# Early planes for two back projections, cumulative decay rows read back from DRAM, and 128-row first tiles in a two-block fp32 layer

## The reference

```python
def first_block(x, w_in, b_f, conv_w, pool_w, pool_scale, w_out, ln_g, ln_b):
    proj = jnp.einsum('bsd,de->bse', x, w_in[l])          # 2048 -> 7176 columns
    (q, k, v, g_att, fg, c_b, c_c, c_h, g_conv, p_u, g_pool) = jnp.split(proj, IN_SPLITS, axis=-1)
    y_att  = forgetting_attention(q, k, v, fg, b_f) * silu(g_att)   # 8 heads of 128, logits + cum_q - cum_k
    y_conv = short_conv_mixer(c_b, c_c, c_h, conv_w) * silu(g_conv)
    y_pool = multiscale_pool_mixer(p_u, pool_w, pool_scale) * silu(g_pool)
    y = jnp.einsum('bse,ed->bsd', concatenate([y_att, y_conv, y_pool]), w_out[l])
    return layer_norm(DEEPNORM_ALPHA * x + y, ln_g, ln_b)

def second_block(x, ...):
    u = jnp.einsum('bsd,de->bse', h, w_in[layer])
    q, k, v, z_attn, q_idx, k_idx, w_idx, z_ssd, xbc, dt_raw = _split_cols(u, IN_WIDTHS_2)
    o_attn = _dsa_attention(q, k, v, q_idx, k_idx, w_idx) * silu(z_attn)   # top-128 keys by an index score
    o_ssd  = _ssd_mixer(xbc, z_ssd, dt_raw, ...)                           # 16 heads in 4 groups, chunks
    sub = jnp.einsum('bse,ed->bsd', concatenate([o_attn, o_ssd]), w_out[layer])
    return layer_norm(DEEPNORM_ALPHA_2 * h + sub, ln_g, ln_b)
```

## Time and profile before

| | |
|---|---|
| median of 3 runs (1828.44 to 1828.81) | 1828.46 us |
| profiled execution: time, span | 1829.15 us, 1827.4 us |
| PE busy | 1764.4 us, 97% of the span |
| PE weight loads busy | 1415.2 us, 77% |
| DVE / ACT / POOL busy | 1002.7 / 574.9 / 714.4 us |
| mean granted TensorE clock | 0.991 of full speed |
| chain that ended last: PE / DVE / ACT | 75% / 20% / 2% |
| DMA | 175.55 MB, 96 GB/s |

### The profile page before, as it was taken

How to read it: one execution, slowest core, us unless ns; L and a number is a source line. 1 busy time by engine, 2 the same in 40 slices (tenths; PEclk the granted TensorE clock), 3 DMA queues, 4 the chain that set the end, 5 groups by cost and what they waited for, 6 DMA issues and landing times.

```text
span 1827.4 us, 22151 instructions
## 1 busy us (share of the span) xinstructions
PE 1764.4 (97%) x7938; PEld 1415.2 (77%) x7938; DVE 1002.7 (55%) x1382; ACT 574.9 (31%) x796; POOL 714.4 (39%) x303
## 2 busy tenths in 40 slices
PE   7999999999999999999899999999989999999996
PEld 6877778788888887888778777777748777778885
DVE  4344333333322645113678989897599766576326
ACT  5322222322222224123632333333362323251211
POOL 3433333343444444443344324343314333325445
PEclk9999999999999999999899999999999999999998
DMA  5322222222333323332433222232212222217422
GB/s 200 114 81 81 81 82 92 81 81 81 99 103 92 97 95 131 116 126 69 163 93 114 69 70 93 62 88 81 69 36 92 81 69 69 80 58 252 126 83 92
DMA packets 50091, 175.55 MB, mean 96 GB/s; under 512 B 5217, under 2 KB 5473, under 8 KB 48865
## 3 DMA queue, kind: packets, MB, share of 16 engines
q1 hardware_dynamic: 41472, 152.13, 26.8%
q10 hardware_dynamic: 8544, 22.37, 3.4%
HBM read 166.09 MB, written 8.39 MB: 95 GB/s over the span
## 4 chain that ended last, share of the span: by engine, by line
PE 75%; DVE 20%; ACT 2%; issue 2%; POOL 1%; DMA 0%; ACTq 0%; DVEq 0%; SPq 0%; POOLq 0%
PE bank L330 73%; DVE gate L1065 3%; DVE feats L1053 2%; DVE bias L1053 2%; DVE bias L1553 1%; PE bank L334 1%; DVE top L1549 1%; DVE probs L1053 1%; DVE gT L1415 1%; DVE gate L1097 1%; DVE nmax L1092 1%; DVE tmp L1053 1%; DVE probs L1104 1%; DVE wide L1408 1%; POOL w_lo L308 1%
## 5 line engine op out<-in xcount | busy, mean ns | idle before, releaser
L308 POOL TENSOR_TENSOR w_lo<-raw,w_hi 128x1024 fp32r<-128x1024 f32 x280 | 688.8, 2464 | 1096.7 <-ACT w_hi L718 1096.7
L330 PE MATMUL bank<-planes_hi,w_hi 128*128 128x512 f32 (+1 forms) x1792 | 709.7, 396 | 19.0 <-DVE w_lo L1128 9.4
L330 PE MATMUL bank<-planes_lo,w_hi 128*128 128x512 f32 (+1 forms) x1792 | 694.8, 388 | 0.0
L330 PE MATMUL bank<-planes_hi,w_lo 128*128 128x512 f32 (+1 forms) x1776 | 687.7, 387 | 0.0
L718 ACT ACTIVATE w_hi<-raw 128x1024 fp32r<-128x1024 f32 x280 | 296.9, 1060 | 909.6 <-PE bank L330 893.3
L330 PEld LDWEIGHTS bank<-planes_hi,w_hi 128*128 128x128 f32 x1792 | 339.7, 190 | 110.2 <-issue 36.6
L330 PEld LDWEIGHTS bank<-planes_lo,w_hi 128*128 128x128 f32 x1792 | 340.1, 190 | 70.2 <-issue 4.8
L330 PEld LDWEIGHTS bank<-planes_hi,w_lo 128*128 128x128 f32 x1776 | 336.2, 189 | 68.3
L330 PE MATMUL bank<-w_hi,planes_hi 128*128 128x512 f32 x512 | 199.9, 391 | 4.2 <-DVE planes_lo L1069 4.2
L330 PE MATMUL bank<-w_hi,planes_lo 128*128 128x512 f32 x512 | 199.2, 389 | 0.0
L330 PE MATMUL bank<-w_lo,planes_hi 128*128 128x512 f32 x512 | 199.2, 389 | 0.0
(11 more groups left out here) (252 smaller groups left out, 1376.5 us busy)
## 6 DMA issues: line engine op xcount, KB each, us to landing
raw<-in_stream SPq DMA_DIRECT2D x282, 512.0 KB, 3.6
h_rows<-feats ACTq DMA_DIRECT2D x4, 1024.0 KB, 7.0
feats<-in_x_t SPq DMA_DIRECT2D x3, 1024.0 KB, 10.5
bias<-in_x_rows ACTq DMA_DIRECT2D x2, 1024.0 KB, 6.2
probs<-in_x_rows ACTq DMA_DIRECT2D x2, 1024.0 KB, 8.4
bias<-h_rows ACTq DMA_DIRECT2D x2, 1024.0 KB, 6.7
probs<-h_rows ACTq DMA_DIRECT2D x2, 1024.0 KB, 8.0
out<-feats ACTq DMA_DIRECT2D x6, 256.0 KB, 2.9
```

The lines of the kernel that those rows point to most:

```text
L308: nc.gpsimd.tensor_sub(w_lo[:, s, :], raw[:, s, :], w_hi[:, s, :].bitcast(fp32)).then_inc(lo_ready, 1)
L330: return nc.tensor.matmul(o, a, b, start=start, stop=stop)
```

## The change

Five things.

1. `EARLY = 4`: ACT cuts the first four planes of each back projection while PE is in the last forward tile before it (`cut_early`), and DVE their low parts.
2. In block 1 the `cum` matrix is stored to DRAM once, and ACT issues a DMA per head that reads the head's row into all 128 partitions (`load_cum_row`). The matmul that spread it and DVE's masking are gone; `logit_bias` reads SBUF.
3. The misc tile and SSD tile 0 are made in parts of 128, 128 and 256 tokens (`project_part`).
4. Of the four transposed banks per row block ACT scales three, DVE one.
5. `prepare` runs after SSD tile 2 and the decay spread after tile 3, both with what DVE does for them; its rows are in `bias`, not in `probs`.

The head loop of block 1 on ACT and the last turn of that of block 2 on ACT and DVE are written out. Lines are those of the diff's two sides; what is left out repeats these edits or only adds and renames semaphores.

```diff
-BACK_ORDER = [list(range(12)) + [15, 14, 13, 12], list(range(8, 16)) + list(range(8))]
+BACK_ORDER = [list(range(12)) + [15, 14, 13, 12], list(range(4)) + list(range(8, 16)) + list(range(4, 8))]
+EARLY = 4
...
-            def turn_and_spread(h):
+            def turn_head_v(h):
                 pe.wait_ge(acc_taken, T_HEAD1 + 4 * h + 3)
                 turn_v(M, vT)
-                pe.wait_ge(cum_row_ready, h + 1)
-                if h:
-                    pe.wait_ge(feat_done, h)
-                mm(O[:, :], ones[0:HEADS, :], cum_row[0:HEADS, :]).then_inc(cum_spread, 1)
...
             pe.wait_ge(rows_taken, 14)
-            project_half(tile_at(T_MISC, 0), 0, T_MISC - SK - 1)
+            project_part(tile_at(T_MISC, 0), 0, 1, T_MISC - SK - 1)
             turn_rows(2)
-            project_half(tile_at(T_SSD, 0), 0)
+            project_part(tile_at(T_SSD, 0), 0, 1)
+            project_part(tile_at(T_MISC, 0), 1, 1)
             turn_rows(3)
-            project_half(tile_at(T_MISC, 0), 1)
-            project_half(tile_at(T_SSD, 0), 1)
+            project_part(tile_at(T_SSD, 0), 1, 1)
+            project_part(tile_at(T_MISC, 0), 2, 2)
+            project_part(tile_at(T_SSD, 0), 2, 2)
...
                 ssd_tile(6 * it + 1)
-                if g < 0:
-                    prepare()
-                else:
+                if g >= 0:
                     ssd_states(g)
                     ssd_spread(g, 0)
                 ssd_tile(6 * it + 2)
                 if g < 0:
-                    spread_decay()
+                    prepare()
...
+            def load_cum_row(a):
+                act.dma_start(cum_rows, cum_dram[a:a + 1, :].to_broadcast([P, S])).then_inc(cum_loaded, 16)
...
+            def cut_early(blk, first):
+                act.wait_ge(unit_used, 2 * first - 1)
+                act.wait_ge(feat_done, 24 * blk + EARLY)
+                for n in range(EARLY):
+                    cut_hi(BACK_ORDER[blk][n], 16 + 32 * blk + n + 1)
...
-            act.wait_ge(cum_ready, 1)
+                if j == 1:
+                    act.wait_ge(cum_ready, 1)
+                    act.dma_start(cum_dram, cumT[0:HEADS, :]).then_inc(cum_stored, 16)
+                if j == 2:
+                    act.wait_ge(cum_stored, 16)
+                    load_cum_row(0)
             exp_gate(1)
-            with step.loop(1, HEADS, 0) as h:
+            for h in range(1, HEADS):
                 head_exps(h - 1)
+                load_cum_row(h)
...
-                        if b < 2:
+                        if b < 3:
                             act.wait_ge(rows_turned, n)
...
-            back_and_norm(0, T_BACK1, x_rows, {1: lambda: turn_round(tile_at(T_POOL, 7))})
+            back_and_norm(0, T_BACK1, x_rows, {EARLY: lambda: turn_round(tile_at(T_POOL, 7))})
...
                 t = tile_at(T_HEAD2, 1, h, 2)
-                turn_round(t)
+                if isinstance(h, int):
+                    round_unit(t[0] + 1, 2 * t[1])
+                    cut_early(1, T_BACK2)
+                    round_unit(t[0] + 1, 2 * t[1] + 1)
...
             def logit_bias(a):
-                dve.wait_ge(cum_spread, a + 1)
+                dve.wait_ge(cum_loaded, 16 * (a + 1))
                 for i in range(QB):
                     n = P * (i + 1)
-                    step(stt(bias[:, i, 0:n], O[:, 0:n], cumN[:, i, at(a)], causal[:, S - n:S], SUB, ADD))
+                    step(stt(bias[:, i, 0:n], cum_rows[:, 0:n], cumN[:, i, at(a)], causal[:, S - n:S], SUB, ADD))
...
+            head2(HEADS - 1)
+            cut_back(1, 0, EARLY)
+            head_finish(2 * HEADS - 2, HEADS - 2, 23 + HEADS)
             a = 2 * HEADS - 1
-            cut_back(1, 0, 2)
+            cut_back(1, EARLY, 5)
             head_softmax(a)
-            cut_back(1, 2, 4)
+            cut_back(1, 5, 6)
+            head_scale(a)
+            cut_back(1, 6, 7)
             head_gate(24)
-            cut_back(1, 4, 5)
-            head_scale(a)
-            cut_back(1, 5, 7)
+            cut_back(1, 7, 8)
             head_take_turned(a)
```

More of the change, by code:

```diff
@@ L115, in block_kernel @@
     h_rows = nc.dram_tensor("h_rows", [S, D], fp32, kind="Internal").ap()
+    cum_dram = nc.dram_tensor("cum_dram", [HEADS, S], fp32, kind="Internal").ap()
     with ExitStack() as ctx:
@@ L373, in project, with project_part @@
                         between()
-            def project_half(tile, half, acc_before=None):
+            def project_part(tile, row, rows, acc_before=None):
                 m, p = tile
@@ L379, in project_half @@
                     pe.wait_ge(acc_taken, acc_before)
-                tokens = slice(256 * half, 256 * half + 256)
+                tokens = slice(P * row, P * (row + rows))
                 for u in range(2):
                     s = 2 * p + u
-                    if half == 0:
+                    if row == 0:
                         pe.wait_ge(lo_ready, 4 * m + s - 3)
@@ L387, in project_half @@
                         if e % 4 == 0:
-                            pe.wait_ge(planes_ready, 32 + 4 * (2 * half + 1) + e // 4 + 1)
+                            pe.wait_ge(planes_ready, 32 + 4 * (row + rows - 1) + e // 4 + 1)
                         hi, lo = w_hi[:, s, P * k:P * k + P], w_lo[:, s, P * k:P * k + P]
@@ L392, in project_half @@
                         last = mm(ACC[p][:, tokens], lo, planes_hi[:, e, tokens], False, e == KT - 1)
-                    if half == 1:
+                    if row + rows == QB:
                         last.then_inc(unit_used, 1)
@@ L822, in back_and_norm @@
                 act.wait_ge(feat_done, 16 * blk + 15)
-                for n in range(KT):
+                for n in range(EARLY, KT):
                     if n == KT - 1:
@@ L932, in _ @@
             take(tile_at(T_MISC, 0), gT[:, :], T_MISC - SK + 1)
-            R = [probs[0:SSD_HEADS, k, :] for k in range(4)]
+            R = [bias[0:SSD_HEADS, k, :] for k in range(4)]
             act.wait_ge(prep_turn, 1)
@@ L1028, in _, with head_tiles2 @@
             exp_gate(17)
-            with step.loop(1, HEADS, 0) as h:
+            def head_tiles2(h):
                 head_exps(HEADS + h - 1)
@@ L1499, in _ @@
                 if it == 0:
[L1500 removed]
+                    take_prepared()
                 if it >= 1:
@@ L1569, in _, with head2 @@
             rope_head(0)
-            with step.loop(1, HEADS, 17) as h:
+            def head2(h):
                 a = HEADS + h - 1
```

81 lines of the change are left out of this document (45 added, 36 removed).

## The result

| | before | after |
|---|---|---|
| median, 20 runs each (least to most) | 1828.45 us (1826.98 to 1830.0) | 1831.45 us (1830.45 to 1833.63) |
| ratio after / before, 95% interval | | 1.0017 [1.0011, 1.0023] |
| profiled span | 1827.4 us | 1828.7 us |
| PE busy | 1764.4 us | 1765.4 us |
| PE weight loads busy | 1415.2 us | 1425.6 us |

The forecast was 9 us faster. The kernel became 3.0 us slower: 0.17%. The ratio's interval excludes 1, but the size is under the 0.2% that the prediction called no change, and it is certainly not the gain forecast. A near zero here isn't a change without effect: a large gain and two large losses cancel. I start with the waits of PE in the changed kernel (who is waited for: total, times, longest, in us).

A forecast was written before the change was run, and what follows sets the result against it. PE was taken as the bound, busy 1764.4 of 1827.4 us. 1829.15 - 8.4 - 3.25 - 3.27 + 4.3 + 1.4 = 1819.9, less 0.69 for the median: 1819.2, say 1819 us; own range 1815 to 1824, chance 0.66.

The forecast's parts named there:

- no change: Whole kernel: a measured time within 0.2% (3.7 us) of the kernel before; chance 0.05.
- part 2, decay rows: Block 1's 8 heads: PE loses a spreading matmul of 1.05 us each, the replacing DMA costs no wait; -8.4 us.
- part 1, early planes: Both back projections: PE's waits for planes and related waits go; -3.25 us in block 1, -3.27 in block 2.
- parts 3 and 4: Handover: narrower matmuls cost more than the shorter waits and slow clock save; misc rows 2-3 end at 909.8 against 905.5, +4.3 us.
- part 5: Preparation around SSD tile 2: the transposes, formerly inside PE's idle, cost their time behind the tile; DVE's copies cost nothing; +1.4 us.
- The price per matmul: Handover: an fp32r matmul of 128 columns with a new stationary operand takes 0.12 us, 5.8 us per part.
- the cost of the change of kind behind the spread: Block 1's heads: the late start of the tile's first matmul behind the transposes stays in both kernels, so only 1.05 us goes.
- its two waits in block 1: First back projection: PE's waits for the first low plane (2.30 us) and the pooling window's input (0.95) both go; -3.25 us.
- those forecast in block 2: Second back projection: the first-plane wait (1.85 us) and four waits in head 7's `head_turn` (1.42 together) go; -3.27 us.
- 0.067 us: Rival at the handover: weight loads overlap, so a 128-column matmul costs 0.067 us; 1812.5 us in all; chance 0.10.
- 0.22 at full clock: Rival at the handover: narrow matmuls run at plain fp32's rate, 0.22 us each, 10.6 per part; 1838 us in all; chance 0.18.
- the early planes gained: Opposite of a rival: early planes gain nothing because POOL's subtraction keeps DVE waiting at both places; 1825.7 us; chance 0.06.

The follow-up runs named there:

- part 2 alone: The kernel before with only the decay rows read back from DRAM; 1818.07 us, ratio 0.9946.
- part 1 alone: The kernel before with only the early planes; 1820.02 us, ratio 0.9957.
- 1819.35: The changed kernel with only the preparation and decay spread put back to their earlier places; 1819.35 us, ratio 0.9953 to the kernel before.
- 1810.11: The kernel before with only the early planes and the decay rows from DRAM; 1810.11 us, ratio 0.9900.
- part 3 alone: Misc tile and SSD tile 0 made in 128-row parts, added to the kernel with early planes and DRAM decay rows; 1815.98 us.
- part 4 alone: ACT scaling three banks and DVE one, added to the kernel with early planes and DRAM decay rows; 1811.99 us.

## Why the prediction was wrong

| step | forecast us | by the trace | by the runs |
|---|---|---|---|
| part 2, decay rows | -8.4 | -10.0 | -10.1 |
| part 1, early planes | -6.5 | -8.2 | -8.4 |
| parts 3 and 4 | +4.3 | +6.6 at SSD tile 1, +8.5 at tile 2 | +9.2 |
| part 5 | +1.4 | +2.1 up to SSD tile 3, +10.5 behind it | +12.1 |

The column of runs is, from above: part 2 alone; part 1 alone (each against its own batch's kernel before); 1819.35 less 1810.11; 1831.45 less 1819.35. It adds up to +2.8, and +3.0 was measured. In the third row part 3 alone cost 5.9 and part 4 alone 1.9, both on top of parts 1 and 2; that leaves 1.4 of the 9.2 to the two together, or to the spread. The measured time lies outside the forecast's own range of 1815 to 1824, and inside the 0.2% of no change, to which the prediction gave 0.05.

**The step that failed** is in the paragraph on part 5: "DVE's five copies move with it and stay in its own time; were DVE the bound in the SSD stage, it would be late by 4.3 plus 1.3, the same." I asked what the copies cost DVE, and whether DVE as a whole was late. I didn't ask what stands ahead of them in DVE's queue, nor who waits for them. They were moved past three `silu_tile`s of 10.0 to 12.5 us each, while their consumer, PE's spread, was moved past one tile of 11 us. The kernel before had everything for it: there the last copy is done at 926.01, ahead of DVE's first SSD tile, and PE's spread comes 12.7 us after that.

```profile
925.79 0.22 DVE L1364 COPY widxN<-bank 128x64 f32<-128x64 f32 x1
926.05 2.48 DVE L1384 TENSOR_SCALAR probs<-padded,par 128x512 f32<-128x512 f32 x1
```

The changed order puts three tiles of DVE, 32.6 us (918.99 to 951.60), ahead of the copies, and one tile of PE, 11 us, ahead of the spread. No rival of the prediction had this wait. Its price was 7.18 us of idle and about 3 of slow clock behind it. The 2.1 us before it are the transposes, 1.33 us (933.26 to 934.59, where I took 1.4), and SSD tile 2, which took 0.9 us longer than before behind its longer wait (919.74 to 933.26, against 926.07 to 938.67).

**Parts 3 and 4** had the right sign and less than half the size. The price per matmul, on which the forecast was to fall, was right: 0.112 us at full clock (two rows at 886.22 and 886.33) where I took 0.12. The first failing term is the clock. I let misc row 0 be slow for 3 us as in the kernel before. Its first 17 matmuls were 0.11 us apart, but from 863.5 on it was slow to its end and through the transposes, for 10.3 us:

```profile
862.00:874.00 12.00, 12.00 (x67) 12.00 (x66) 4.28 (x8) 11.00 (x23) 6.86 (x3) 0.57 0.39 131
874.00:884.00 10.00, 10.00 (x92) 10.00 (x92) 4.12 (x8) 4.34 (x11) 0.00 (x0) 1.00 0.19 54
```

Misc row 0 took 8.6 us, from 861.65 to 870.27, against 7.2 forecast, and `turn_rows(2)` 3.3 us against 1.6: together 3.1 us. The start gained 0.6 us less than forecast, and the rest up to SSD tile 1 took 1.4 less (29.5 us against 30.9); so 2.3 us too little were forecast up to there. The other 1.9 came between SSD tiles 1 and 2. They go to the second failing term, part 4's 1.48 us of ACT per row block: I followed it to the weights of SSD tile 0 and no further, and it came out again in the preparation chain. From the start of SSD tile 1 to that of tile 2 PE took 14.8 us in the kernel before and with parts 1 and 2, 14.4 with part 3 added, but 16.8 with part 4 added, and 16.8 with all parts but 5.

**Part 2** was right, and short by 0.2 us a head: I kept the cost of the change of kind behind the spread, but the transposes alone, 0.36 us to the next product, leave almost none of it. The DMA was no wait. It landed in 3.3 us:

```profile
rope_q<-cum_dram ACTq DMA_DIRECT2D x8, 256.0 KB, 3.3
```

The bias operations did get slower, 977 ns on average against 551, and hid as forecast behind DVE's idle time. The mean hides that only the first of each head's four did. The groups of one shape, before and after:

```profile
L1053 DVE SCALAR_TENSOR_TENSOR bias<-bank,cumN,rope_q 128x128 f32<-128x128 f32 x8 | 2.8, 351 | 4.3 <-PE bank L330 4.3
```

```profile
L1084 DVE SCALAR_TENSOR_TENSOR bias<-rope_q,cumN 128x128 f32<-128x128 f32 x8 | 16.4, 2053 | 4.2 <-DVE vN L1150 4.2
```

The three wider ones kept their 0.49, 0.62 and 0.75 us. In head 1 the slow one ran from 109.23 to 111.16, while POOL's subtraction ran from 108.63 to 111.02.

**Part 1** gained its two waits in block 1 (-3.66 against -3.25) and more than those forecast in block 2 (-4.5 against -3.27). Of the rivals none came true: the narrow matmuls cost neither 0.067 us nor 0.22 at full clock (0.21 only at the low one), and the early planes gained. The Trainium skill (TensorE: Matmul & The Clock Gate, Back-to-back issue gap) says about 81 ns for a stream of such matmuls; 112 were measured for fp32r, so its figure doesn't hold here. What did hold is the bound from the weight loads' lengths, 0.106.

## What to carry to other kernels

When a step is moved, follow each of its results on each engine: what stands ahead of it in the queue now, and when its reader asks. A copy of 0.22 us waits for all the work ahead of it in the queue, however idle the engine is on average: here the first copy started 17 us after its input was ready (951.64 against 934.6). A stage split finer to start earlier paid here per instruction and not per column, and about double while the clock was low behind a gap. Work moved forward on one engine can start another engine's work beside a third's: twice here ACT rounded weights earlier, POOL subtracted earlier, and DVE slowed down beside it. When several edits come together, measure each alone, since here a kernel 18.5 us faster lay inside one that was 3 us slower.

## What the runs showed of the hardware

- fp32r matmuls with a new 128x128 weight each, start to start: 0.112 us for 128 columns and 0.12 for 256 at 2.4 GHz; both 0.21 at 1.2 GHz. Going from 256 columns to 128 saved nearly nothing.
- Behind the first wait of the handover (3.1 to 5.0 us) PE ran at the 1.2 GHz level for 3.1 to 4.8 us in the nine kernels without part 3, and for 10.2 to 13.6 us in the five with it, without idle time in either. What makes the difference wasn't isolated.
- From the first of four plain transposes to the next fp32r product took 0.36 us. With one plain matmul of 512 columns between them it took 1.58: 1.22 more, where the matmul's start and the product's start are 1.05 apart.
- DVE operations beside POOL's subtraction of weights took longer: four scans 5.88 us in place of 1.75, the scaling of half a row block 2.60 in place of 0.81, the first bias operation of a head 2.05 in place of 0.35 on average (that one also reads SBUF in place of PSUM). The traces show the two at the same time; no run kept the one and took the other away.
